# Last two gate tiles by token halves, and the final norm and output laid out anew, in a one-core decoder layer

## The reference, cut to what matters

```
x = x + 0.5 * swiglu(rms_norm(x, g_ffn2), w1_ffn2, w3_ffn2, w2_ffn2)
gate = jax.nn.sigmoid(rms_norm(x, g_ple) @ w_ple_gate)
x = x + gate * (ple @ w_ple_proj)
...
y = rms_norm(x, g_final)      # over the 1024 features of each token
```

## Time and profile before

| what | value |
|---|---|
| median of 3 runs | 996.93 us |
| the profiled execution, its own time | 998.08 us |
| its span, from first to last instruction | 996.3 us |
| mean granted PE clock over the span | 0.995 |
| PE busy | 971.6 us (98% of the span) |
| DVE, ACT, POOL busy | 673.2, 456.6, 278.3 us |
| output transfers after the last gate tile | 8 of 256 KB and one of 32 KB, all issued by SP |

### The profile page before, as it was taken

The page is one execution under the profiler, slowest core; times in us unless marked ns, Lnnn a source line. Parts: engine busy times, 40 slices in busy tenths (PEclk is TensorE's granted clock), DMA queues, the critical chain, the costliest instruction groups (busy, mean ns, idle before and its releaser), DMA issues.

```text
span 996.3 us, 19264 instructions
## 1 busy us (share of the span) xinstructions
PE 971.6 (98%) x7965; PEld 956.7 (96%) x7965; DVE 673.2 (68%) x999; ACT 456.6 (46%) x742; POOL 278.3 (28%) x155
## 2 busy tenths in 40 slices
PE   6999999999999999999999999999999999999996
PEld 5999999999999999999989999999999999999995
DVE  5799657856768563456875399757756758755575
ACT  6644424532544444555434455434543444445132
POOL 2303202211111226321448412301311111215461
PEclk9999999999999999999999999999999999999998
DMA  7952433252243327221114693243324224234202
GB/s 213 165 122 73 129 96 104 67 159 66 63 128 106 96 75 206 76 64 43 44 54 128 127 170 96 75 127 96 96 87 126 85 64 138 79 111 140 73 14 86
DMA packets 192178, 101.38 MB, mean 102 GB/s; under 512 B 13018, under 2 KB 189492, under 8 KB 192076
## 3 DMA queue, kind: packets, MB, share of 16 engines
q1 hardware_dynamic: 176624, 90.76, 32.1%
q0 software_dynamic: 11440, 5.77, 4.7%
q10 hardware_dynamic: 4028, 3.63, 1.2%
HBM read 97.59 MB, written 3.59 MB: 102 GB/s over the span
## 4 chain that ended last, share of the span: by engine, by line
PE 89%; DVE 5%; DMA 2%; ACT 2%; POOL 1%; issue 1%; SPq 0%; DVEq 0%; ACTq 0%
PE ps L1612 52%; PE ps L1692 32%; DMA w_raw<-in_w_ffn_dram 1%; PE ps L1648 1%; POOL h_lo L1061 1%; PE ps L1929 1%; DMA x_rows<-in_x_prompt_dram 1%; PE ps L1902 1%; DVE ab L1325 0%; ACT w_hi L693 0%; ACT h_hi L800 0%; PE ps L1643 0%; DVE mix_lo L1499 0%; DVE rs_t L1143 0%; DVE xb_lo L1177 0%
## 5 line engine op out<-in xcount | busy, mean ns | idle before, releaser
L1692 PE MATMUL ps<-xo_lo,w_hi 128*128 128x260 f32 x1008 | 284.7, 282 | 0.0
L1692 PE MATMUL ps<-xo_hi,w_lo 128*128 128x260 f32 x1008 | 284.4, 282 | 0.0
L1692 PE MATMUL ps<-xo_hi,w_hi 128*128 128x260 f32 x1008 | 284.2, 282 | 0.0
L1612 PE MATMUL ps<-h_hi,w_hi 128*128 128x260 f32 x960 | 195.8, 285 | 2.0 <-POOL h_lo L1061 1.2
L1612 PE MATMUL ps<-h_lo,w_hi 128*128 128x260 f32 x960 | 193.6, 283 | 0.0
L1612 PE MATMUL ps<-h_hi,w_lo 128*128 128x260 f32 x960 | 193.6, 283 | 0.0
L1692 PEld LDWEIGHTS ps<-xo_hi,w_lo 128*128 128x128 f32 x1008 | 189.8, 188 | 0.0
L1692 PEld LDWEIGHTS ps<-xo_lo,w_hi 128*128 128x128 f32 x1008 | 189.7, 188 | 0.0
L1692 PEld LDWEIGHTS ps<-xo_hi,w_hi 128*128 128x128 f32 x1008 | 189.6, 188 | 0.0
L1054 POOL TENSOR_TENSOR w_lo<-w_a,w_hi 128x512 fp32r<-128x512 f32 x36 | 66.8, 1857 | 307.6 <-ACT w_hi L762 307.6
L1612 PEld LDWEIGHTS ps<-h_hi,w_hi 128*128 128x128 f32 x960 | 148.2, 189 | 3.6 <-issue 3.4
(11 more groups left out here) (253 smaller groups left out, 1436.5 us busy)
## 6 DMA issues: line engine op xcount, KB each, us to landing
w_raw<-in_w_ffn_dram SPq DMA_DIRECT2D x88, 256.0 KB, 3.0
w_a<-in_w_ffn_dram SPq DMA_DIRECT2D x36, 512.0 KB, 4.9
w_raw<-in_w_ffn_dram SPq DMA_DIRECT2D x48, 384.0 KB, 3.5
w_raw<-in_w_ffn_dram SPq DMA_DIRECT2D x16, 512.0 KB, 6.1
w_lo<-in_w_ffn_dram POOLq DMA_DIRECT2D x11, 512.0 KB, 9.4
w_raw<-in_w_in_dram SPq DMA_DIRECT2D x10, 512.0 KB, 4.0
w_raw<-in_w_ple_gate_dram SPq DMA_DIRECT2D x8, 512.0 KB, 3.9
x_rows<-in_x_prompt_dram SPq DMA_DIRECT2D x4, 512.0 KB, 5.5
```

The source lines that it names most:

```text
L1612: ins = pe.matmul(ps[:, bank + step * h, 0:HALF], w[:, c, w0:w0 + P], m_[:, sk, h * HALF:(h + 1) * HALF], start=(first and n == 0), stop=( ...
L1692: ins = pe.matmul(ps[:, b, 0:Q], w[:, c, k * P:(k + 1) * P], m_[:, op, k, :], start=(first and k == 0 and n == 0), stop=(k == 3 and n == 2 ...
```

## The change

The change does five things.

1. The gate tiles 6 and 7 are computed by token halves of 256 and 264 tokens, in the order (6, first), (7, first), (6, second), (7, second). This holds for PE (`half_unit`), for DVE and ACT (`LAST_HALVES`), and for the squares; POOL adds three of the four half squares, and the last, (7, second), stays in `sq`.
2. The sums of squares: PE sums `ssq` for the five blocks as soon as POOL has added the third half, and `sq` only for the blocks 2, 3 and NB. That makes 8 products in two parts where there were 10 in one.
3. All transposes now stand behind the last gate product. Their banks are `Y_BANKS`, and the sums of squares lie in bank 7 instead of 0.
4. SP sends the blocks 1 and 0 as one transfer of 512 KB each, after both halves of a block are ready, then block 2 in two halves and the samples. ACT issues the two halves of block 3 on its own queue, after its last multiplication.
5. DVE's multiplication of the samples is still its last, and ACT's wait for the turned samples is for the second count of `y_turned`.

```diff
-STAT_BANK = (None, 7, 7, 7, 0)
-Y_PAIR = (3, 2, 0, 1, 1)
+STAT_BANK = (None, 7, 7, 7, 7)
+Y_BANKS = ((4, 5), (6, 0), (1, 2), (3, 7), (1, 2))
+LAST_CUT = ((0, 256), (256, 520))
+LAST_HALVES = ((KD - 2, 0), (KD - 1, 0), (KD - 2, 1), (KD - 1, 1))
...
@@ sync
-            for blocks in ((1, 0), (3, 2)):
-                for h in range(2):
-                    for b in blocks:
-                        sp_.wait_ge(y_ready[b], h + 1)
-                        sp_.dma_start(o["y_prompt"][0, b * P:(b + 1) * P, h * 512:(h + 1) * 512],
-                                      y[:, b, h * 512:(h + 1) * 512]).then_inc(out_done, 16)
+            for b in (1, 0):
+                sp_.wait_ge(y_ready[b], 2)
+                sp_.dma_start(o["y_prompt"][0, b * P:(b + 1) * P, :], y[:, b, :]).then_inc(out_done, 16)
+            for h in range(2):
+                sp_.wait_ge(y_ready[2], h + 1)
+                sp_.dma_start(o["y_prompt"][0, 2 * P:3 * P, h * 512:(h + 1) * 512],
+                              y[:, 2, h * 512:(h + 1) * 512]).then_inc(out_done, 16)
...
@@ scalar
-            for m in range(KD):
+            for m in range(KD - 2):
...
+            for i, (m, h) in enumerate(LAST_HALVES):
+                t = slice(*LAST_CUT[h])
+                act.wait_ge(gated, KD - 2 + i)
+                act.wait_ge(z_ready, KD - 2 + i + 1)
+                nc.scalar.activation(tb[:, t], ta[:, t], ACT.Tanh, scale=0.5).then_inc(gate_ready, 1)
+                act.wait_ge(sq_added, 28 + KD - 2 + (0, 1, 1, 3)[i])
+                act.wait_ge(x_ready, 24 + KD - 2 + i + 1)
+                nc.scalar.activation(sq[:, t], x[:, m, t], ACT.Square).then_inc(sq_made, 1)
...
+            for h in range(2):
+                act.wait_ge(y_ready[3], h + 1)
+                act.dma_start(o["y_prompt"][0, 3 * P:4 * P, h * 512:(h + 1) * 512],
+                              y[:, 3, h * 512:(h + 1) * 512]).then_inc(out_done, 16)
...
@@ gpsimd
+            for i, (m, h) in enumerate(LAST_HALVES[:3]):
+                t = slice(*LAST_CUT[h])
+                pool.wait_ge(sq_made, 24 + KD - 2 + i + 1)
+                pool.wait_ge(sq_added, 28 + KD - 2 + i)
+                nc.gpsimd.tensor_tensor(ssq[:, t], ssq[:, t], sq[:, t], ALU.add).then_inc(sq_added, 1)
...
@@ tensor
+            for m, h in LAST_HALVES:
+                half_unit(m, h).then_inc(unit_done if h else first_half, 1)
...
             pe.wait_ge(rstd_ready, 8)
-            pe.wait_ge(xf_ready, KD - 1)
-            pe.wait_ge(z_ready, KD - 1)
-            for b in (0, 1):
-                turn_back(b, range(KD - 1))
+            pe.wait_ge(sq_added, 28 + KD - 2 + 3)
+            for b in range(NB + 1):
+                sum_of(ssq, b, b == 0, b < 2)
+            pe.wait_ge(xf_ready, KD)
             pe.wait_ge(z_ready, KD)
-            turn_back(NB, range(KD - 1))
-            pe.wait_ge(xf_ready, KD)
-            for b in (NB, 0, 1):
-                turn_back(b, (KD - 1,)).then_inc(y_turned, 1)
-
-            pe.wait_ge(sq_added, 9 * 4 - 1)
-            pe.wait_ge(sq_made, 8 * 4)
-            for b in range(NB + 1):
...
+            turn_back(0, range(4))
+
+            pe.wait_ge(sq_made, 24 + KD + 2)
+            for b in (2, 3, NB):
+                ins = sum_of(sq, b, False, True)
             ins.then_inc(stat_summed, 1)
+            turn_back(0, range(4, KD)).then_inc(y_turned, 1)
+            pe.wait_ge(xf_ready, KD + 2)
+            pe.wait_ge(z_ready, KD + 2)
+            turn_back(NB, range(KD)).then_inc(y_turned, 1)
+            turn_back(1, range(KD)).then_inc(y_turned, 1)
             pe.wait_ge(sums_taken, 1)
+            turn_back(3, range(KD)).then_inc(y_turned, 1)
+            pe.wait_ge(ys_taken, 1)
             turn_back(2, range(KD)).then_inc(y_turned, 1)
-            pe.wait_ge(ys_taken, 1)
-            turn_back(3, range(KD)).then_inc(y_turned, 1)
```

More of the change, by code:

```diff
@@ L1003, in _ @@
                 nc.scalar.activation(sq[:], x[:, m, :], ACT.Square).then_inc(sq_made, 1)
-            act.wait_ge(y_turned, 1)
+            for i, (m, h) in enumerate(LAST_HALVES):
[6 more added lines that the diff above has]
+                nc.scalar.activation(sq[:, t], x[:, m, t], ACT.Square).then_inc(sq_made, 1)
+            act.wait_ge(y_turned, 2)
             nc.scalar.activation(xf_rows[0:TS, :].rearrange("p (a c) -> p a c", a=2),
-                                 ps[0:TS, 2 * Y_PAIR[NB]:2 * Y_PAIR[NB] + 2, :], ACT.Copy).then_inc(ys_taken, 1)
+                                 ps[0:TS, Y_BANKS[NB][0]:Y_BANKS[NB][0] + 2, :], ACT.Copy).then_inc(ys_taken, 1)
             act.wait_ge(rs_ready, 1)
-            for b in (1, 3):
-                act.wait_ge(y_turned, b + 2)
+            for b, turned in ((1, 3), (3, 4)):
+                act.wait_ge(y_turned, turned)
                 for h in range(2):
-                    nc.scalar.activation(y[:, b, h * 512:(h + 1) * 512], ps[:, 2 * Y_PAIR[b] + h, :],
+                    nc.scalar.activation(y[:, b, h * 512:(h + 1) * 512], ps[:, Y_BANKS[b][h], :],
                                          ACT.Copy, scale=rs[:, b:b + 1]).then_inc(y_ready[b], 1)
+            for h in range(2):
+                act.wait_ge(y_ready[3], h + 1)
+                act.dma_start(o["y_prompt"][0, 3 * P:4 * P, h * 512:(h + 1) * 512],
+                              y[:, 3, h * 512:(h + 1) * 512]).then_inc(out_done, 16)
         @block.gpsimd
@@ L1587, in _ @@
                 nc.vector.tensor_scalar(xf[:, m, :], x[:, m, :], col(C_FIN + m), None, ALU.mult).then_inc(xf_ready, 1)
+            for i, (m, h) in enumerate(LAST_HALVES):
+                t = slice(*LAST_CUT[h])
+                n = LAST_CUT[h][1] - LAST_CUT[h][0]
+                count = KD - 2 + i
+                dve.wait_ge(gate_ready, count)
+                if h == 0:
+                    dve.wait_ge(first_half, i + 1)
+                else:
+                    dve.wait_ge(unit_done, done[("gate", m)])
+                nc.vector.tensor_tensor(ta[:, t], ps[:, 2 * (m % 3) + h, 0:n], rstd[:, t], ALU.mult).then_inc(z_ready, 1)
+                dve.wait_ge(gate_ready, count + 1)
+                nc.vector.scalar_tensor_tensor(out=tq[:, t], in0=tb[:, t], scalar=1.0, in1=pp[:, m, t], op0=ALU.add,
+                                               op1=ALU.mult).then_inc(gated, 1)
+                dve.wait_ge(gated, count + 1)
+                nc.vector.scalar_tensor_tensor(out=x[:, m, t], in0=tq[:, t], scalar=0.5, in1=x[:, m, t], op0=ALU.mult,
+                                               op1=ALU.add).then_inc(x_ready, 1)
+                dve.wait_ge(x_ready, 24 + count + 1)
+                nc.vector.tensor_scalar(xf[:, m, t], x[:, m, t], col(C_FIN + m), None, ALU.mult).then_inc(xf_ready, 1)
@@ L1590, in _ @@
             stat_rsqrt(4)
             nc.vector.tensor_copy(rs_t[:], rs[:]).then_inc(rs_ready, 1)
-            for b in (0, 2):
-                dve.wait_ge(y_turned, b + 2)
+            for b, turned in ((0, 1), (2, 5)):
+                dve.wait_ge(y_turned, turned)
                 for h in range(2):
-                    nc.vector.tensor_scalar(y[:, b, h * 512:(h + 1) * 512], ps[:, 2 * Y_PAIR[b] + h, :],
+                    nc.vector.tensor_scalar(y[:, b, h * 512:(h + 1) * 512], ps[:, Y_BANKS[b][h], :],
@@ L1596, in _ @@
                                             rs[:, b:b + 1], None, ALU.mult).then_inc(y_ready[b], 1)
[L1597 to L1600, removed]
+            dve.wait_ge(ys_taken, 1)
+            nc.vector.tensor_scalar(y[0:TS, NB, :], xf_rows[0:TS, :], rs[0:TS, NB:NB + 1], None,
+                                    ALU.mult).then_inc(y_ready[NB], 1)
@@ L2010, in _ @@
             stat_sum(3)
-            for m in range(1, KD):
+            for m in range(1, KD - 2):
                 if m < 3:
@@ L2016, in _, with half_unit @@
                 unit(("gate", m), xg[3], m % 3, between=[(6, lambda: stat_out(3))] if m == 1 else ())
+            def half_unit(m, h):
+                key = ("gate", m)
+                c0, c1 = LAST_CUT[h]
+                if h == 0:
+                    lo_wait(pe, key)
+                    pe.wait_ge(z_ready, m - 2)
+                for k in range(KD):
+                    c, w0 = cell[key] + k // 4, k % 4 * P
+                    for n, (w, m_) in enumerate(((wh, xb_hi), (wh, xb_lo), (wl, xb_hi))):
+                        ins = pe.matmul(ps[:, 2 * (m % 3) + h, 0:c1 - c0], w[:, c, w0:w0 + P], m_[:, k, c0:c1],
+                                        start=(k == 0 and n == 0), stop=(k == KD - 1 and n == 2))
+                return ins
+            for m, h in LAST_HALVES:
+                half_unit(m, h).then_inc(unit_done if h else first_half, 1)
             def turn_back(b, ks):
@@ L2021, in turn_back, with sum_of @@
                 for k in ks:
-                    ins = pe.transpose(ps[0:n, 2 * Y_PAIR[b] + k // 4, (k % 4) * P:(k % 4 + 1) * P],
+                    ins = pe.transpose(ps[0:n, Y_BANKS[b][k // 4], (k % 4) * P:(k % 4 + 1) * P],
```

(10 more changed lines are left out.)

6 lines of the change are left out of this document (3 added, 3 removed).

## The result

The changed kernel takes 1001.37 us, the median of 19 executions (998.71 to 1003.34), and the kernel before 998.93, the median of 19 on the same chips (996.17 to 1000.25). The ratio is 1.0028, with a 95% interval of 1.002 to 1.0036: 2.8 us slower (the two medians lie 2.4 us apart). The forecast was 997.6 (996.1 to 999.5) and no change that can be measured. Two things put the number outside: the three runs that I started from were low by 2.0 us, and the move was 2.4 us between the medians, 2.8 by the ratio, where I had summed 0.7.

The account below looks back on a forecast made before the run. It took PE to bound the kernel up to the last gate product, then a chain of waits to the first output issue. First issue 989.3 plus 7.7 gave 997.0 against 996.3, +0.7 on the median 996.93: 997.6 us (996.1 to 999.5).

Parts of the forecast that it names:

- (b): PE's sums of squares before the inverse root: -1.1 us at full clock, -0.1 us with the expected clock fall.
- rival B: Full clock until block 1 is turned: first issue at 988.2, -0.4 us, 996.5 us; chance 0.17.
- (a): Token halves of tiles 6 and 7 through DVE and ACT, up to the last square: no gain, +0.2 us.
- the collision with POOL's addition: On DVE, POOL's adding of tile 5's square delays the first half: 975.69, its x done at 976.16.
- (c): The inverse root on DVE: the same 15 instructions, 2.75 us, ending at 987.65.
- (d): Turning blocks, ACT's first block and first output issue: the larger transfer waits for two halves, issue at 989.3, +0.7 us.
- (e): Output transfers from first issue to the end: same DMA rate, 7.7 us, change 0.
- rival D: Output moves faster with 4 KB rows and two queues, kernel faster by over 0.2%; chance 0.07.
- C: Clock low from the sums to the end of turning: first issue +3.6 or +2.6 us, 1000.5 or 999.5; chance 0.21.

Follow-up runs that it names:

- with the gap filled: Changed kernel plus 24 unused products of 256 columns in PE's idle stretch behind the last gate product; ratio 0.9988 against the kernel before.
- the kernel before with split sums: Kernel before with the sums of squares in two parts, five of them between the transposes, without token halves; ratio 0.9986.
- the one with the output of before: Changed kernel with the earlier nine output transfers, all on SP, each issued when its half block is ready; ratio 1.0015 against the kernel before.
- late transposes: Kernel before with 24 transposes (blocks NB, 0 and 1) moved behind the sums and nothing else changed; ratio 1.0035.
- the one with new output: Kernel before with only the change's output transfers: blocks 1 and 0 as 512 KB each, block 3 issued by ACT; ratio 1.0002.
- the halves with early transposes: Kernel before with token halves, blocks 0 and 1 transposed right behind the last gate product, 8 sums in one piece; ratio 1.0007.

## Why the prediction was wrong, by its own steps

**The step that failed** is in (b): "For what PE loses by it I take what it loses now: 11 transposes at 0.24 instead of 0.115, 1.4 us". That the clock would fall, that it would fall within or just behind the sums, and that an idle stretch of nearly 3 us does it, was right (3.00 us, where I had 2.7). But I took the low stretch of before as the size of the new one. There it began among transposes and lasted 3.4 us; after the change it begins at the sums and lasts 6.8, with PE busy all through. Of my 1.4 us, 1.0 was used up by the end of the sums, which left 0.4 for the 20 transposes up to the end of block 1. Measured, the last transpose of block 1 begins 10.0 us behind the last gate product, and 7.2 with the gap filled: PE loses 2.7 to 2.8 us by then, not 1.4. The inverse root hides a part of it, and at the first issue the clock costs 2.4 us (11.8 against 9.4 with the gap filled), where my sum had 1.1 (989.3 against 988.2, the issue of rival B).

- **(a)** +0.2 us forecast, +0.5 measured. The groups on DVE came 2.16 to 2.18 us apart (2.14 forecast) and the collision with POOL's addition held the first half to 976.72, on time. ACT took 0.42 us for a half, not 0.39, and POOL 0.74, not 0.65. The halves pay nothing, as said.
- **(b)** -1.1 at full clock forecast; with the gap filled -0.8 (5.2 against 6.0). In the changed kernel 0.0, against a forecast of -0.1. The price of a sum at half clock, taken as double (0.46), was measured as 0.43.
- **(c)** 2.75 us, as forecast (985.95 to 988.70).
- **(d)** I had ACT at block 1 beside the root, 8.8 us behind the last product. It was 10.5: this is where the missing stretch of low clock shows. The larger first transfer costs 0.6 us at the first issue (10.2 against 9.6 in the kernel before), 0.7 forecast, and 0.4 at the end.
- **(e)** 7.7 us from the first issue to the end, 7.5 measured. The DMA rate for rows of 4 KB is the same, which ends rival D.

Among the rivals, C named what happened: low from the sums until block 1 is turned, with the first issue later by more than 2.0 us. I gave it 0.21. Its size was "+3.6", or "+2.6" with the clock back for block 1; the clock wasn't back for block 1, and yet it was 2.2, since the first five sums still ran at 1.00 and the root began 6.0 us behind the last gate product, not 6.9. The one argument against C, the return of the clock behind transposes alone at 989.6, was read as a promise of an early return. It said only that a return is possible, and nothing of when. It came with PE idle since 988.9, and behind the same 16 transposes in the kernel before with split sums the clock didn't come back at all within the span:

```profile
986.50:987.00 0.50, 0.50 (x5) 0.50 0.00 0
...
990.00:990.50 0.50, 0.00 (x0) 0.50 1.03 381
...
995.50:996.00 0.50, 0.00 (x0) 0.50 0.01 0
```

(The columns are PE busy, the granted clock, the share of the DMA engines and GB/s.) The middle of bounds 4.0 us apart was no forecast, and the side to lean to was the one that the gap pointed to.

The number was off for another reason as well: 996.93 came from three executions, and 19 gave 998.93. By the measured ratio alone the kernel would have come out at 999.7 from my base, 0.2 beyond the range, and from the base of 998.93 the range would have ended at 1001.5, just above the 1001.37 measured. So the base made a part of the miss, and the low clock the rest.

## What to carry to other kernels

Work that PE does while it waits is not free to be moved just because it isn't on the chain: it may be what keeps the clock up for the work behind it. Before moving it, look at the granted clock on both sides of the gap that the move opens, and price all that follows at both levels, not only as much of it as is slow today. Here the useful part of a five-part change was one that could be had alone, the sums in two parts, placed so that they fill the wait instead of emptying it.

## What the runs showed of the hardware that I had not expected

- How long the granted clock stayed low didn't follow from how busy PE was. It was low for 6.8 us where its fall came at or just behind the first sums (changed kernel twice, the one with the output of before, late transposes), though PE was busy without a gap from the fall on. It was low for 3.4 us where the fall came among the last 16 transposes in the kernel before, in the one with new output, and in the halves with early transposes (986.9 to 990.3), and for 10 us, up to the end of the span, in the kernel before with split sums, where the fall came among the same transposes. What sets the length isn't shown by these runs.
- Filled with 24 transposes, a wait holds the clock as well as with 24 products: 1.00 in every stretch up to the end of the transposes.
- A product by one column, with 128 columns of weights, isn't of fixed cost: 0.22 us at full clock, 0.43 at half. Its price follows the clock.
- Half a tile isn't half a price on ACT and POOL: 0.42 us where the whole took 0.64, and 0.74 where it took 1.31.
